# A two-layer decoder trunk on one core: a later compress step, a matmul moved into an out tile, and the last centring on TensorE

## What is computed

```python
h = jnp.einsum('btd,de->bte', x, w_in)
...
kc = compress(k_cmp_all, cmp_pe[0], cmp_w[0])
vc = compress(v_cmp_all, cmp_pe[1], cmp_w[1])
kc = partial_rope(kc, kc_end)
...
y = jnp.einsum('btd,de->bte', merged, w_out)
out = layer_norm(ALPHA * x + y, ln_g, ln_b)      # (x - mean) * rsqrt(var + eps) * g + b
```

## Time and profile before

| what | value |
|---|---|
| median of 3 executions | 773.47 us (772.49 to 773.5) |
| span of the profiled execution | 770.6 us |
| PE busy | 750.7 us, 97% of the span |
| DVE, ACT, POOL busy | 566.9, 404.7, 130.8 us |
| mean granted TensorE clock | 0.996 |

### The profile page before, as it was taken

The page is one execution under the profiler, slowest core; times in us unless marked ns, Lnnn a source line. Parts: engine busy times, 40 slices in busy tenths (PEclk is TensorE's granted clock), DMA queues, the critical chain, the costliest instruction groups (busy, mean ns, idle before and its releaser), DMA issues.

```text
span 770.6 us, 16973 instructions
## 1 busy us (share of the span) xinstructions
PE 750.7 (97%) x6302; PEld 703.4 (91%) x6302; DVE 566.9 (74%) x1015; ACT 404.7 (53%) x805; POOL 130.8 (17%) x222
## 2 busy tenths in 40 slices
PE   8999999999999999999999989999999999999994
PEld 7997898988889999999869989988988999999993
DVE  4475689998779575665774687999977876766676
ACT  5544277666556444444445455865655563444452
POOL 2331014331100033100600000444011000000033
PEclk9999999999999999999999999999999999999998
DMA  8988456666845688765528774666667455656531
GB/s 315 295 286 263 127 165 182 204 220 220 293 161 169 187 249 276 239 175 181 167 87 249 236 228 146 196 191 208 220 231 282 129 176 185 181 176 189 174 129 56
DMA packets 42938, 154.94 MB, mean 201 GB/s; under 512 B 6640, under 2 KB 7664, under 8 KB 42096
## 3 DMA queue, kind: packets, MB, share of 16 engines
q1 hardware_dynamic: 33952, 115.55, 47.9%
q0 software_dynamic: 8912, 38.37, 14.9%
HBM read 145.77 MB, written 13.34 MB: 206 GB/s over the span
## 4 chain that ended last, share of the span: by engine, by line
PE 84%; DVE 11%; issue 2%; DMA 2%; ACT 1%; SPq 0%; DVEq 0%
PE bank L732 22%; PE bank L733 22%; PE bank L734 22%; PE bank L750 4%; DVE w_lo L1305 2%; PE bank L960 2%; DMA ring<-weights_dram 2%; DVE probs L1520 2%; PE bank L743 1%; PE bank L1001 1%; PE bank L901 1%; DVE probs_t L1535 1%; PE bank L895 1%; PE bank L931 1%; DVE u_max L1495 1%
## 5 line engine op out<-in xcount | busy, mean ns | idle before, releaser
L732 PE MATMUL bank<-x_hi,w_hi 128*128 128x264 f32 x1208 | 350.1, 290 | 1.4 <-DVE w_lo L1305 1.4
L1305 DVE TENSOR_TENSOR w_lo<-ring,w_hi 128x1024 fp32r<-128x1024 f32 x202 | 247.9, 1228 | 136.1 <-ACT w_hi L1103 132.4
L734 PE MATMUL bank<-x_lo,w_hi 128*128 128x264 f32 x1208 | 342.7, 284 | 0.0
L733 PE MATMUL bank<-x_hi,w_lo 128*128 128x264 f32 x1208 | 342.4, 283 | 0.0
L1103 ACT ACTIVATE w_hi<-ring 128x1024 fp32r<-128x1024 f32 x202 | 213.9, 1060 | 54.8 <-DMA ring<-weights_dram 27.1
L732 PEld LDWEIGHTS bank<-x_hi,w_hi 128*128 128x128 f32 x1208 | 227.6, 188 | 5.6 <-issue 3.3
L733 PEld LDWEIGHTS bank<-x_hi,w_lo 128*128 128x128 f32 x1208 | 227.8, 189 | 0.4
L734 PEld LDWEIGHTS bank<-x_lo,w_hi 128*128 128x128 f32 x1208 | 226.8, 188 | 0.0
L732 PE MATMUL bank<-h_rounded,w_hi 128*128 128x264 f32 x352 | 100.3, 285 | 0.2
L733 PE MATMUL bank<-h_rounded,w_lo 128*128 128x264 f32 x352 | 100.2, 285 | 0.0
L1155 ACT ACTIVATE h<-bank 128x264 f32<-128x264 f32 x88 | 35.1, 398 | 75.6 <-PE bank L734 70.0
(11 more groups left out here) (273 smaller groups left out, 1052.4 us busy)
## 6 DMA issues: line engine op xcount, KB each, us to landing
ring<-weights_dram SPq DMA_DIRECT2D x208, 512.0 KB, 4.0
cache_a<-kcmp_dram POOLq DMA_DIRECT2D x32, 128.0 KB, 4.1
cache_b<-vcmp_dram POOLq DMA_DIRECT2D x32, 128.0 KB, 3.9
cache_a<-ksel_dram POOLq DMA_DIRECT2D x32, 128.0 KB, 3.3
cache_b<-vsel_dram POOLq DMA_DIRECT2D x32, 128.0 KB, 3.2
kwin_out_dram<-kwin_dram POOLq DMA_DIRECT2D x8, 512.0 KB, 4.1
vwin_out_dram<-vwin_dram POOLq DMA_DIRECT2D x8, 512.0 KB, 6.0
cache_a<-kwin_dram POOLq DMA_DIRECT2D x2, 2048.0 KB, 11.4
```

What stands on the lines that cost most here:

```text
L732: pe.matmul(out, w_high[:, k0 + k, :], high, start=(k == 0), stop=False)
L733: pe.matmul(out, w_rest[:, k0 + k, :], high, start=False, stop=False)
L734: ins = pe.matmul(out, w_high[:, k0 + k, :], rest, start=False, stop=(k == kn - 1))
L1305: dve.tensor_tensor(w_lo[:, slot % RING], ring[:, slot % RING], w_hi[:, d % HI_RING].bitcast(F32), ALU.subtract).then_inc(w_lo_ready, 1)
```

## The change

Three moves, each with its signals:

- In layer two `cmp_rope` stands behind place 19 and `cmp_sum 1` keeps place 18.
- In both layers the shift's matmul is issued inside out 2, before its k tile 2 (`SHIFT_AT = 2`), and no longer ahead of out 2. What ACT does at the step `shift` is unchanged and stays at its place.
- At the end of layer two a step `centre` is added ahead of `norm`: PE makes z - mean for tiles 4 to 7 in four banks, by three matmuls each (identity with z, then -1/1024 with z_sum and with z tile 7). DVE scales tiles 4 and 5 straight from their banks, with no centring of its own. ACT copies tiles 6 and 7 out of their banks and POOL scales them. ACT applies gain and bias to tiles 0 to 4 only, and DVE to 5, 6 and 7.

```diff
-    {13: [("cmp_k", 0)], 14: [("cmp_v", 0)], 16: [("cmp_sum", 0)], 18: [("cmp_rope", 0), ("cmp_sum", 1)]})
+    {13: [("cmp_k", 0)], 14: [("cmp_v", 0)], 16: [("cmp_sum", 0)], 18: [("cmp_sum", 1)], 19: [("cmp_rope", 0)]})
...
-        return order + [("mean", 0), ("square", 6), ("square", 7), ("norm", 0)]
+        return order + [("mean", 0), ("square", 6), ("square", 7), ("centre", 0), ("norm", 0)]
...
-                else:
-                    sp.wait_ge(last_ready, 1)
+                if k >= KT8 // 2 - 2:
+                    sp.wait_ge(last_ready, k - KT8 // 2 + 3)
                 sp.dma_start(y_out[:, part, :], m[:, part, :]).then_inc(y_stored, 16)
...
+            pool.wait_ge(rstd_ready, DEPTH)
+            for n in (KT8 - 2, KT8 - 1):
+                pool.wait_ge(last_centred, n - KT8 + 3)
+                go()
+                pool.tensor_tensor(z[:, n, :], z[:, n, :], rstd[:, :], ALU.mult).then_inc(pool_scaled, 1)
...
+                        def shift_at(k):
+
+                            if k == SHIFT_AT:
+                                wait_emptied(pe, l, "out", 0)
+                                pe.matmul(bank[SA][:, 0:T], ones[:, :], z[:, 0, :], start=True, stop=True
+                                          ).then_inc(shift_sum, 1)
...
-                            product(out_bank(step, i)[:, 0:T], w, merge_tile).then_inc(slots_done, 1)
+                            product(out_bank(step, i)[:, 0:T], w, merge_tile, ready=shift_at if i == 2 else None
+                                    ).then_inc(slots_done, 1)
...
+                    elif step == "centre":
+                        for j in range(4):
+                            out = out_bank(step, i, j)[:, 0:T]
+                            pe.matmul(out, ident, z[:, 4 + j, :], start=True, stop=False)
+                            pe.matmul(out, less_ones[:, :], z_sum, start=False, stop=False)
+                            done(pe.matmul(out, less_ones[:, :], z[:, KT8 - 1, :], start=False, stop=True), step, i, j)
...
-                        for n in range(KT8 - 2 if l == DEPTH - 1 else KT8):
+                        if l == DEPTH - 1:
+                            for n in (KT8 - 2, KT8 - 1):
+                                wait_filled(act, l, "centre", 0, n - 4)
+                                act.activation(z[:, n, :], bank[FILL[l, "centre", 0, n - 4][0]][:, 0:T], ACT.Copy
+                                               ).then_inc(last_centred, 1)
+                        for n in range(KT8 - 3 if l == DEPTH - 1 else KT8):
...
-                            if k == 2:
+                            if k == 2 and l < DEPTH - 1:
                                 center(4, 4)
-                                dve.wait_ge(centered, 2 * l + (3 if l == DEPTH - 1 else 2))
+                                dve.wait_ge(centered, 2 * l + 2)
+                            if l == DEPTH - 1 and k == 3:
+                                continue
+                            if l == DEPTH - 1 and k == 2:
+                                for n in (2 * k, 2 * k + 1):
+                                    wait_filled(dve, l, "centre", 0, n - 4)
+                                    src = bank[FILL[l, "centre", 0, n - 4][0]][:, 0:T]
+                                    ins = dve.tensor_tensor(z[:, n, :], src, rstd[:, :], ALU.mult)
+                                ins.then_inc(scaled, 1)
+                                continue
...
-                            for n in (KT8 - 2, KT8 - 1):
+                            for n in range(KT8 - 3, KT8):
+                                if n > KT8 - 3:
+                                    dve.wait_ge(pool_scaled, n - KT8 + 3)
                                 ins = dve.tensor_scalar(m[:, n, :], z[:, n, :], pr("ln_g", n, 1), pr("ln_b", n, 1),
                                                         ALU.mult, ALU.add)
```

More of the change, by code:

```diff
@@ L173 @@
 COPIES = 4
+SHIFT_AT = 2
 Y_PARTS = [(CB, Y_B_HI, 4), (PU, Y_A_HI, 4)] + [(Q + 2 * n, Y_C_HI + 2 * n, 2) for n in range(4)]
@@ L227, in banks_of @@
         return [OT] if i else []
-    return {"v_new": [OT], "cmp_k": [SA, SB], "gates": [MI],
+    return {"v_new": [OT], "cmp_k": [SA, SB], "gates": [MI], "centre": [PT0, PT1, OT, MI],
             "cmp_v": [OT, PT0], "cmp_rope": [MI],
@@ L283 @@
 ROPE_Z = [0, 2, 0, 2, 4, 6]
-VECTOR_STEPS = 100
+VECTOR_STEPS = 99
 def trunk(nc, x_in, weights, params, consts, pages, kcmp, vcmp, ksel, vsel, kwin, vwin,
@@ L325, in trunk @@
         ones = sb("ones", [P, P])
+        less_ones = sb("less_ones", [P, P])
         eps = sb("eps", [P, 1])
@@ L456, in trunk @@
         z_summed, squares_summed = sem("z_summed"), sem("squares_summed")
+        rstd_ready, last_centred, pool_scaled = sem("rstd_ready"), sem("last_centred"), sem("pool_scaled")
         mean_squared, var_ready = sem("mean_squared"), sem("var_ready")
@@ L562, in _ @@
             pool.memset(p_cmp[:, :], 0.0)
+            pool.memset(less_ones[:, :], -1.0 / D_MODEL)
             pool.wait_ge(landed[RING - 1], 16)
@@ L1078, in _ @@
                                         ins.then_inc(slots_done, 1)
-                    elif step == "shift":
-                        wait_emptied(pe, l, "out", 0)
-                        pe.matmul(bank[SA][:, 0:T], ones[:, :], z[:, 0, :], start=True, stop=True).then_inc(shift_sum, 1)
                     elif step == "square":
@@ L1296, in _ @@
                                 ins = act.activation(x_hi[:, n, :], z[:, n, :], ACT.Identity, bias=pr("ln_b", n, 1))
-                            if n % 2:
+                            if n % 2 or l == DEPTH - 1 and n == KT8 - 4:
                                 ins.then_inc(output_ready if l == DEPTH - 1 else x_hi_ready, 1)
@@ L1739, in _ @@
                         dve.wait_ge(std_ready, l + 1)
-                        link(dve.reciprocal(rstd[:, :], rstd[:, :]))
+                        dve.reciprocal(rstd[:, :], rstd[:, :]).then_inc(rstd_ready, 1)
+                        dve.wait_ge(rstd_ready, l + 1)
                         dve.wait_ge(state_stored, (l + 1) * 16)
                         for k in range(4):
-                            if k == 2:
+                            if k == 2 and l < DEPTH - 1:
                                 center(4, 4)
-                                dve.wait_ge(centered, 2 * l + (3 if l == DEPTH - 1 else 2))
+                                dve.wait_ge(centered, 2 * l + 2)
[8 more added lines that the diff above has]
+                                continue
                             if l == DEPTH - 1:
@@ L1757, in _ @@
                         if l == DEPTH - 1:
[L1758 to L1759 removed]
+                            dve.wait_ge(scaled, l * 4 + 3)
+                            for n in range(KT8 - 3, KT8):
+                                if n > KT8 - 3:
+                                    dve.wait_ge(pool_scaled, n - KT8 + 3)
                                 ins = dve.tensor_scalar(m[:, n, :], z[:, n, :], pr("ln_g", n, 1), pr("ln_b", n, 1),
                                                         ALU.mult, ALU.add)
[L1762 removed]
+                                if n != KT8 - 2:
+                                    ins.then_inc(last_ready, 1)
                             break
```

## The result

The changed kernel takes 775.31 us (median of 11 executions, 774.09 to 776.41), the kernel before 773.0 (11 executions, 770.91 to 774.91). The ratio is 1.0027, with a 95% interval of 1.0016 to 1.0037: by the ratio 2.1 us slower (the two medians lie 2.3 us apart). One of the three moves made the kernel faster, the two others made it slower.

A forecast was written before the change was run, and what follows sets the result against it. PE was busy 750.7 of 770.6 us, so only its waits or work behind its last product could pay. Compress -1.0, shift -0.33 and 0, end +0.8 made -0.5: 773.47 to 772.95 us, 8-in-10 range 771.7 to 774.2.

The forecast's parts named there:

- before ACT's 768.0 and hidden behind it: End of layer two: POOL's scalings end at 766.3 and DVE's output of tile 7 at 766.7, ahead of ACT's last tile.
- The +0.8 us: End of layer two: later issue of part 2 and three stores close together make the end 0.8 us later.
- 0.33 in layer one and 0 in layer two: Shift's matmul inside out 2: 0.33 us gained in layer one, nothing in layer two.
- The 0.33 goes, in each layer: Shift: the wait and restart at its matmul, 0.33 us, vanish because its operand is long there inside out 2.
- 0.4 us later: Shift in layer two: its sum is ready for ACT at 740.17 where ACT took it at 739.77 before.
- a wait of PE at the mean: Layer two's end: PE waits over z_sum because POOL's chain moves by 0.4 us, using up the shift's 0.33.
- the weight of place 21: Layer two's compress: DVE has it made at 462.74, in time for PE's product by 0.15 us.
- The term of 1.0 us: Layer two's compress: PE gains 1.0 us of the 1.98 us wait; half of the wait moves to cmp_scores.
- POOL last: Rival at the end: POOL's scalings take 1.75 us each, tying with ACT at 773.0, or 773.95 if its chain lengthens; chance 0.08.
- The compress gives nothing: Rival in layer two's compress: a later wait takes back PE's gain, total +0.5 us, 773.95; chance 0.15.
- the end pays after all: Rival at the end: centring matmuls at twice the pace, end -1.0, total 770.8; chance 0.12 with mixtures.
- Slower: Rival at the end: clock falls to 1.2 GHz while PE centres, end 5.4 us late, 777.6; chance 0.07.

The follow-up runs named there:

- end_dve_scales: As end_only, but DVE instead of POOL scales tiles 6 and 7 behind ACT's copies; ratio 1.0012 to the kernel before.
- late_pool: Kernel before plus one unused 128x128 memset on POOL, released when DVE has scaled the last tiles; ratio 1.0037, 2.9 us slower.
- less_late_pool: Kernel before plus the same POOL memset as late_pool, released when DVE has scaled the first pair of tiles; ratio 1.0006.
- shift_5: As shift_only, but the shift's matmul stands ahead of k tile 5 of out 2; ratio 1.0059 to the kernel before, 4.6 us slower.
- shift_only: Kernel before with only the shift's matmul moved inside out 2, ahead of k tile 2, in both layers; ratio 1.0026, 2.0 us slower.
- end_only: Kernel before with only the end move: centring on PE, copies on ACT, scaling on POOL and DVE; ratio 1.003, 2.3 us slower.
- compress_only: Kernel before with only cmp_rope one place later in layer two; ratio 0.9975, 1.9 us faster.
- warm_wait: Kernel before plus four unused matmuls on PE ahead of its wait at cmp_rope in layer two, cmp_rope at its old place; ratio 0.9982, 1.4 us faster.

## Why the prediction was wrong, by its own steps

**The end: one term was left out.** The step of the prediction that failed is the one that calls POOL's part at the end "before ACT's 768.0 and hidden behind it": it counted the two scalings and stopped there. POOL's instructions don't end with its last scaling but with the closing DRAIN of 6.3 to 6.8 us, and every engine waits for it. It was in the trace of before, in the rows of the program's last line, and the prediction didn't read them. end_dve_scales takes POOL's work away and gives back 1.7 us; late_pool adds one memset and pays 2.9 (3.5 in its trace); less_late_pool adds it 3 us earlier and pays nothing that its times can tell. The other terms of the end were right: twelve matmuls 0.44 us apart, ACT the engine that ends last, the stores in a row. The +0.8 us is what end_dve_scales shows (10.2 against 9.4 us); no run divides it between the later issue and the stores standing closer.

**The shift: the sign was wrong.** The prediction gave 0.33 in layer one and 0 in layer two. Two steps failed. "The 0.33 goes, in each layer": it doesn't, since out 2 writes the bank of out 0 (the out tiles alternate between two banks), so its first matmul waits for the very copy that the shift waited for, 0.26 us, seen in the waits of the changed kernel. And "0.4 us later" for ACT was 0.8, because this wait stayed ahead of the shift's matmul. What is queued behind ACT's copy was followed to POOL's chain, but not back to PE: table load, weight of out 4 on ACT, its rest on DVE, and only then DVE's emptying of out 2, whose bank out 4 needs. PE stood 0.8 us there. The sign that the prediction named for layer two, a wait of PE at the mean, didn't appear. shift_5 fits this: 1.1 us later, 1.1 us more wait. Cost 0.75 us per layer, where -0.33 and 0 were forecast.

**The compress: the mechanism was right, the size depended on the execution.** PE's wait gone, DVE's stretch only permuted, cmp_scores waiting for `kc_bd` 0.8 us: as predicted, but for the weight of place 21, which came late, at no cost. The term of 1.0 us came from one trace, in which PE waited 1.98 us and the granted clock stayed at 1.00. With cmp_rope at its old place the wait was 2.0 to 2.8 us in the seven traces that have it there without more work ahead of it, and in four of them (shift_only, end_only, end_dve_scales, less_late_pool; not in the kernel before, late_pool, shift_5) the granted clock fell to half, between the last 0.6 us of the wait and 1.3 us behind its end, and the products there ran at half pace for 3.4 us (6.8 in end_only). None of the traces with the later place shows it, the changed kernel's included. So the move is worth 1.9 us by the ratio of compress_only.

That the rest is the clock is seen by sorting the executions by their mean granted clock. The profiled execution of the kernel before, in which the clock falls only behind the last product, has 0.996. Beside compress_only the kernel before ran 35 times: 9 executions had 0.996, with a median of 771.95 us, and the 26 others 0.990 to 0.994, with 773.6. Of compress_only's 12 executions 11 had 0.995 or 0.996, with a median of 771.25. So where the clock was kept the move gives about 0.7 us, on few executions and a little under the prediction's 1.0; the rest of the 1.9 is that the fall became rare. warm_wait, which keeps the wait's cause and shortens the idle time, says the same: 1.4 us faster in all (its interval reaches nearly to zero), 11 of 12 executions at 0.995 or 0.996 against 7 of 35 beside it, and no gain over those 7 (772.2 against 771.5 us). The mean of an execution doesn't say where the clock fell; that it is this place rests on the traces.

**The sum.** By the single moves, 0.9975 x 1.0026 x 1.003 = 1.0031, against 1.0027 measured. In microseconds -1.9 + 2.0 + 2.3 = +2.4. The forecast of -0.5 was 2.6 short: 1.7 by the DRAIN, about 1.8 by the shift (1.5 and the 0.33), less 0.9 that the compress gave more. That last part is luck: without the clock, which the prediction didn't count at this place, it would have been further off.

**The rivals.** "POOL last" named the right engine and the wrong reason: the scalings took 0.75 and 0.74 us, with no lengthening by DVE at all. "The compress gives nothing" and "the end pays after all" didn't happen. "Slower" named the clock at PE's centring, where it stayed at full level until 769. The fall of the clock belongs to the other place, and there the change avoids it. A small error beside these: the prediction laid 2.87 us around the span by taking the profiled execution for a median one; it is 2.0 in the changed kernel's, and 1.8 to 1.9 in the executions of the kernel before that list both. The forecast doesn't hang on it.

## What to carry to other kernels

An engine's last work is not its last instruction: read what closes the program on each engine, and count its length from the last operation you give that engine. Before a wait is called removed, list what else the next instruction waits for (here the two banks in turn), and follow whatever is made later round the whole ring of engines until it comes back to the one that is saved. A wait of PE behind which the granted clock falls in some executions is worth more than its own length, and one profile may not show it: look at the mean clock of all executions.

## What the runs showed of the hardware

- POOL's closing DRAIN: 6.35 us where POOL's last work are the sums of squares and in less_late_pool, 6.82 and 6.83 with the two scalings at the very end, 6.40 with a memset. All engines leave the program behind it.
- TensorE's granted clock fell from 2.4 to 1.2 GHz at a stand of PE of 2.0 (end_dve_scales), 2.3 (less_late_pool), 2.7 (shift_only) and 2.8 us (end_only), in end_only 0.6 us before PE's next matmul, in less_late_pool 1.3 us behind it. It stayed down for 3.4 us, in end_only 6.8, with PE at work from its next matmul on. At stands of 2.0 (the kernel before), 2.4 (late_pool) and 2.5 us (shift_5) it didn't fall.
- POOL's operations on 264 columns: 0.75 us for the scaling of tile 6, beside DVE's operations from a PSUM bank; 0.74 for that of tile 7, of which DVE's gain and bias overlap only the first 0.14 us; 1.75 for a sum of squares beside DVE's operation for the rest of a weight, which reads two tiles in SBUF. The Trainium skill, GPSIMD Engine Reference, section Specifications, puts contention with VectorE on its instructions with two SBUF inputs or in a two-port mode; the operations beside the first scaling had one input in a bank, and the trace agrees.
